# Half a product more before the bonus sums, and a decay scan in two pieces, in a two-block kernel on one Trainium2 core

## What is computed

```python
w_log = -jax.nn.softplus(-(w0 + jnp.tanh(pwd) @ w2)) - 0.5
decay = jnp.exp(-jnp.exp(w_log))          # cumulated over 64 tokens at a time by the kernel
a = jax.nn.sigmoid(a0 + pad_ @ a2)
k = pk * (1.0 + (a - 1.0) * k_a)
bonus = jnp.sum(r_h * k_h * r_k, axis=-1, keepdims=True) * v_h
_, sel = lax.top_k(score, topk)           # topk = 256
```

## Time and profile before

| | |
|---|---|
| median of 3 runs | 2707.3 us (2706.68 to 2709.66) |
| the profiled execution, its own time | 2704.38 us |
| its span on the core | 2702.6 us |
| busy PE, DVE, ACT, POOL in the whole span | 95%, 53%, 31%, 35% |
| the stage of the change, from the span's start | about 1567 to 2018 us |
| mean granted clock of PE over the span | 0.981 |

### The profile page before, as it was taken

The page is one execution under the profiler, slowest core; times in us unless marked ns, Lnnn a source line. Parts: engine busy times, 40 slices in busy tenths (PEclk is TensorE's granted clock), DMA queues, the critical chain, the costliest instruction groups (busy, mean ns, idle before and its releaser), DMA issues. The chain is left out here.

```text
span 2702.6 us, 40631 instructions
## 1 busy us (share of the span) xinstructions
PE 2557.4 (95%) x17201; PEld 2085.5 (77%) x17201; DVE 1441.9 (53%) x2106; ACT 849.2 (31%) x1393; POOL 947.9 (35%) x490
## 2 busy tenths in 40 slices
PE   7998999999999999998989999999999998899997
PEld 5887778888888888886867567777776778887786
DVE  5113543343342211223585689999975655565844
ACT  3304463321110111233432453533416541112331
POOL 3212333443342422444444025534512102121664
PEclk9999999999999999999999999999999999999999
DMA  3113213122222111112234014223322001101523
GB/s 130 48 41 109 94 40 108 48 87 82 83 83 93 49 39 50 52 47 86 78 102 148 32 34 131 94 90 121 110 90 97 17 26 71 35 4 58 186 71 109
DMA packets 82086, 207.67 MB, mean 77 GB/s; under 512 B 8393, under 2 KB 21745, under 8 KB 81905
## 3 DMA queue, kind: packets, MB, share of 16 engines
q1 hardware_dynamic: 74992, 192.48, 21.7%
q10 hardware_dynamic: 6912, 12.59, 1.2%
HBM read 170.81 MB, written 35.27 MB: 76 GB/s over the span
## 5 line engine op out<-in xcount | busy, mean ns | idle before, releaser
L332 PE MATMUL ps<-region_rounded,weights_hi_by_slot 128*128 128x512 f32 x2432 | 964.7, 397 | 32.2 <-DVE region_rounded L610 13.3
L333 PE MATMUL ps<-region_rounded,weights_hi_by_slot 128*128 128x512 f32 x2432 | 950.8, 391 | 0.0
L334 PE MATMUL ps<-region_rounded,weights_lo_in_place 128*128 128x512 f32 x2432 | 950.8, 391 | 0.0
L326 POOL TENSOR_TENSOR weights_lo_in_place<-wbuf,weights_hi_by_slot 128x1024 fp32r<-128x1024 f32 x194 | 486.0, 2509 | 735.2 <-ACT weights_hi_by_slot L322 735.2
L332 PEld LDWEIGHTS ps<-region_rounded,weights_hi_by_slot 128*128 128x128 f32 x2432 | 460.2, 189 | 137.3 <-issue 33.4
L333 PEld LDWEIGHTS ps<-region_rounded,weights_hi_by_slot 128*128 128x128 f32 x2432 | 460.1, 189 | 100.4 <-issue 6.1
L334 PEld LDWEIGHTS ps<-region_rounded,weights_lo_in_place 128*128 128x128 f32 x2432 | 459.4, 189 | 96.5
L322 ACT CAST weights_hi_by_slot<-wbuf 128x1024 fp32r<-128x1024 f32 x194 | 201.6, 1043 | 348.0 <-DMA wbuf<-w_mlp 219.5
L2065 DVE MAX8 gcols<-region 128x8 f32<-128x384 f32 (+5 forms) x192 | 171.5, 893 | 6.0
L2067 DVE MATCH_REPLACE8 region<-gcols,region 128x384 f32<-128x384 f32 (+5 forms) x192 | 168.1, 876 | 0.0
L1358 POOL TENSOR_TENSOR region_rounded<-region,region_rounded 128x512 fp32r<-128x512 f32 x64 | 83.1, 1298 | 214.6 <-DVE region_rounded L1502 214.6
(11 more groups left out here) (334 smaller groups left out, 3560.0 us busy)
## 6 DMA issues: line engine op xcount, KB each, us to landing
wbuf<-w_mlp SPq DMA_DIRECT2D x64, 512.0 KB, 3.6
wbuf<-w_hn SPq DMA_DIRECT2D x37, 512.0 KB, 4.0
wbuf<-w_in SPq DMA_DIRECT2D x25, 512.0 KB, 3.7
region<-xT SPq DMA_DIRECT2D x24, 512.0 KB, 6.5
xtra<-w_ada SPq DMA_DIRECT2D x32, 384.0 KB, 4.2
scratch_hn_out<-tmp ACTq DMA_DIRECT2D x48, 256.0 KB, 2.2
region<-scratch_hn_out SPq DMA_DIRECT2D x24, 512.0 KB, 8.2
wbuf<-w_att SPq DMA_DIRECT2D x20, 512.0 KB, 3.6
```

The lines of the kernel that those rows point to most:

```text
L326: self.nc.gpsimd.tensor_tensor(self.m.lo4[:, n % SLOTS, :], self.m.raw4[:, n % SLOTS, :], self.m.hi4[:, n % SLOTS, :].bitcast(F32), ALU.su ...
L332: nc.tensor.matmul(out, m.hi4[:, s, w], m.rounded(hi + k, half(hf)), start=(k == 0), stop=False)
L333: nc.tensor.matmul(out, m.hi4[:, s, w], m.rounded(lo + k, half(hf)), start=False, stop=False)
L334: return nc.tensor.matmul(out, m.lo4[:, s, w], m.rounded(hi + k, half(hf)), start=False, stop=(k == KT - 1))
```

## The change

Four things are done.

1. PE issues the two bonus sums of a program behind half product 8 of its count, not 7. ACT's L2013 and L2015 and POOL's L1887 to L1892 move by one half product too (8 to 9), and so do the stores on SP (9 to 10, 10 to 11).
2. `cumulate` makes two scans, of 896 and 128 columns, where it made 16 of 64. The scan computes state = keep * state + W. `keep` is 1 and is 0 at each 64th column, so the sum starts anew there. It lies in a part of the score area that the six blocks do not use. POOL waits for two scans instead of 16.
3. `keep` is written at the start of the stage by two MEMSETs on DVE, the second one (14 columns, 64 apart) behind a wait for the first.
4. DVE's jobs move to other rounds: clamps of programs 1 to 3 by 1, 2, 2 rounds, the inversions (with the scans) by 2 rounds each, the bonus products of all four by 4, 5, 4, 4 rounds.

```diff
-CLAMP_AT, INVERT_AT, BONUS_AT = [22, 75, 117, 153], [31, 81, 122, 158], [43, 91, 131, 165]
+CLAMP_AT, INVERT_AT, BONUS_AT = [22, 76, 119, 155], [31, 83, 124, 160], [47, 96, 135, 169]
...
+    keep_ready = S("keep_ready")
...
+    LONG = 14 * RL
+    keep = m.flat(SCORES, 4)[:, 25 * P:25 * P + LONG]
...
@@ sync
-                p = group_at(j, 9)
+                p = group_at(j, 10)
                 if p is not None:
                     sp.wait_ge(bonus_out, 2 * (p + 1))
...
-                p = group_at(j, 10)
+                p = group_at(j, 11)
                 if p is not None:
                     sp.wait_ge(rk_ready, p + 1)
...
@@ gpsimd
-                    pool.wait_ge(cum_ready, NC * 2 * (p + 1))
+                    pool.wait_ge(cum_ready, 2 * (p + 1))
...
-                p = group_at(j, 8)
+                p = group_at(j, 9)
                 if p is not None:
                     pool.wait_ge(e2_ready, p + 1)
...
@@ tensor
-                p = group_at(j, 7)
+                p = group_at(j, 8)
                 if p is not None:
                     pe.wait_ge(bonus_in, p + 1)
...
@@ vector
             def cumulate(p):
                 dve.wait_ge(lora_taken, 4 * (p + 1))
+                dve.wait_ge(keep_ready, 2)
                 if p:
                     dve.wait_ge(rb_ready, p)
-                for c in range(2 * NC):
-                    cols = slice(c * RL, (c + 1) * RL)
-                    nc.vector.tensor_tensor_scan(C[:, cols], m.const("ones")[:, 0:RL], W[:, cols], 0.0, ALU.mult, ALU.add
-                                                 ).then_inc(cum_ready, 1)
+                nc.vector.tensor_tensor_scan(C[:, 0:LONG], keep, W[:, 0:LONG], 0.0, ALU.mult, ALU.add).then_inc(cum_ready, 1)
+                nc.vector.tensor_tensor_scan(C[:, LONG:], keep[:, 0:T - LONG], W[:, LONG:], 0.0, ALU.mult, ALU.add
+                                             ).then_inc(cum_ready, 1)
...
             nc.vector.memset(S1[:, 0:1], 0.0).then_inc(consts_ready, 1)
+            nc.vector.memset(keep, 1.0).then_inc(keep_ready, 1)
+            dve.wait_ge(keep_ready, 1)
+            nc.vector.memset(keep[:, 0:LONG:RL], 0.0).then_inc(keep_ready, 1)
```

## The result

The changed kernel takes 2693.84 us, the median of 6 runs (2688.59 to 2694.75), beside 2706.99 us before (6 runs, 2704.14 to 2711.35). The ratio is 0.9942, 95% interval 0.9932 to 0.9952: faster by 0.6%, 13 to 18 us.

What follows compares the result with a forecast made beforehand. PE, busy 95%, was taken as the bound, its four stalls costing 18.4 us; less a 2.4 us wait left in program 3, 16.0 us go: 2707.3 - 16.0 = 2691.3 us, range 2687.5 to 2698.0.

Steps and rivals of the forecast that it cites:

- What a stall costs: PE's four waits before the bonus sums, with slower sums at the lower clock, lose 2.4 + 5.4 + 5.2 + 5.4 = 18.4 us.
- Part 1, the move: PE's bonus sums ask 5.44 us later; all else fixed, no wait is left and 18.4 us go, but lateness needs recomputing.
- The rival "no change": Scans save nothing, PE is tied to program 3, and rounds and L2070 give back the 5.44 won: 2708 us; chance 0.05.
- Part 2, the scans: On DVE, two long scans take 2.3 us with POOL quiet, saving 0.65 us; program 0 takes 4.7, saving 2.6.
- The sign of being wrong: On DVE, the prediction is wrong if long scans take over 2.1 ns a column beside a quiet POOL.
- Part 3, the ledger: PE's lateness by DVE's scans' end: -0.2, -1.0, +2.4 us in programs 1 to 3; PE gains 16.0 us.
- the rival of 10.9 us: DVE's L2070 of 640 columns falls behind POOL's L1890, costing 2.3 us; gain 10.9 us, 2696.4 us; chance 0.22.
- What costs nothing: MEMSETs, about 1.0 us, hide under DVE's 3.99 us wait at the first clamp; later ACT, POOL, SP steps delay nobody.
- The end: At the stage's end PE still finishes last, at 2001.6 us, 3.2 us behind DVE at 1998.4.

Runs made afterwards that it cites:

- the kernel with 158: Changed kernel with program 3's inversion at round 158, not 160: stage 435.56 us, median 2689.11, ratio 0.9930; run again, stage 434.22, median 2692.89, ratio 0.9933.
- the move alone: Kernel before with only the bonus sums' steps on PE, ACT, POOL and SP one half product later: stage 437.92 us, median 2694.16, ratio 0.9948.
- the kernel with the scans alone: Changed kernel with the order and all rounds of before, leaving the two long scans and MEMSETs: stage 448.86 us, median 2699.53, ratio 0.9969.

## Why the prediction was right

- **What a stall costs: right.** 18.4 us were counted from four stalls; with all waits gone the stage is 18.3 us shorter (the kernel with 158). The clock's share was real: only 12.5 of it stood as waits.
- **Part 1, the move: right, and more than I gave it.** I wrote that with all else fixed no wait would be left, but that DVE would not come forward with PE. It does come forward in part without any edit of DVE: its meetings with POOL vanish when POOL runs earlier. I used this for the changed kernel and did not ask what it meant for the move alone. Had the text gone one step further, it would have said that the long scans and the later rounds cancel. The rival "no change" made the same slip: it left the sets of 16 at their old 7.3, 3.0, 7.4 and 5.2 us. In the kernel with 16 scans at the new places they took 7.3, 3.0, 3.0 and 3.0, and the stage was still 7.0 us shorter than before.
- **Part 2, the scans: right in size.** 2.02 and 0.40 us against 2.0 and 0.4; program 0 cost 4.5 against 4.7, with the short scan at 2.55. A set of 16 takes 3.01 us from the first start to the last end, the pair 2.32: 0.69 saved, where the rows had given 0.65. (The rows' 2.07 ns a column give 2.12 us for 1024 columns, not the 2.17 in the sum; it changes nothing.) The sign of being wrong, over 2.1 ns a column, did not show if it is read as the slope, as it was derived: from 8 columns (0.165 us) to 896 (2.02) it is 2.09. The whole duration over its columns is 2.25. The estimate from the 58 cycles per instruction of the Trainium skill ("VectorE: DVE Perf Modes", section on the TRN2 errata) was 0.85; the runs are nearer to the rows.
- **Part 3, the ledger: right at its end, mixed on the way.** Program 3's wait was 2.16 us, 2.3 of lateness; its scans ended 8.65 us earlier than before, said 8.6. Programs 1 and 2 had more room than said: POOL's operand was ready 2.5 and 1.3 us before PE asked (said 0.2 and 1.0). Two meetings that hung on 0.1 us fell the other way: L2076 of 512 columns took 0.43 us, not 2.4, and that of 640 columns 2.60, where I had taken it free. The second is what the rival of 10.9 us was made of, but the first had given DVE 2.0 us and the second took 2.1, so the sum held. Two readings of the ledger were wrong and cancelled: its 0.1 us at program 3 is luck.
- **What costs nothing: right, with a term mis-sized.** The MEMSETs were put at 1.0 us; they cost 3.2. They pushed L2056, at 1572.29, behind the start of POOL's first L326 (1572.21, for 2.39 us), and it took 2.34 us instead of 0.16. Of the cover of 3.99 us at the first clamp 0.79 was left, and nothing of it in the two executions whose start was quicker by 1.6 us (last section). SP's and ACT's later steps held nobody up: PE has no other wait in the stage.
- **The end: right.** DVE ends 3.4 us ahead of PE, said 3.2.

The median is 2.5 us above the forecast. The stage is exact to 0.1, so the difference lies in the rest of the kernel. The same changed kernel reached the stage 1.9 us apart in its three profiled executions and took 3.2 us more or less behind it.

## What to carry to other kernels

A wait that a late operand causes is best priced per occurrence, as old lateness, less the work put in front of it, plus what the waiting engine has gained by then, less what the supplier has gained. The third term is the one that is forgotten, and it is what leaves a wait in the last of four programs that looks like the others. When an edit frees time on an engine off the path, ask what that time is spent on: here two later rounds in each of programs 1 to 3 gave all of it back, and 2.1 us more were to be had by not moving them.

## What the runs showed of the hardware that was not expected

**The clock does not fall at one length of idleness.** In the kernel with the scans alone PE idled 2.79 us and its sums took 1.98 us; it idled 2.67 us in the next program and they took 3.68. The granted clock in the first 2 us of these sums was 1.00 and 0.53. Of the waits before the bonus sums in all twelve profiled executions, all eight of up to 2.16 us kept the clock, and all six of 3.02 and more lost it. A wait of 3.02 us can keep it elsewhere, as the next paragraph shows.

**The stage's start is not always the same length.** After a wait of 3.02 or 3.03 us PE takes 30.60 to 30.65 us to its first head sums in ten of the twelve executions, 29.03 and 29.05 in two. The windows of the changed kernel and of the second one with 158 show the granted clock in the first 6 us:

```profile
1571.00:1577.00 6.00, 5.88 (x19) 4.74 (x20) 5.54 (x11) 1.05 (x1) 2.39 (x1) 0.72 0.07 22
```

```profile
1574.00:1580.00 6.00, 5.84 (x26) 4.85 (x27) 5.49 (x11) 1.13 (x2) 2.42 (x1) 1.00 0.10 25
```

It was 0.72 in the one and 1.00 in the other (and 0.72 and 1.00 over the same 6 us in the other executions too, by their start). The shift of 1.6 us is more than the 0.79 that the MEMSETs had left of DVE's cover: in both quick executions DVE does not wait at its first clamp, comes later than PE would have it, and so in program 0 POOL's L1864 starts before DVE's long scan (0.4 us before it in the kernel with the scans alone). The long scan takes 4.22 us in both, the pair 6.7; it takes 2.02 in every execution with the slower start, in which POOL's L1864 waits for it. POOL's timelines, first the changed kernel, then the one with the scans alone (a quick start):

```profile
1623.19 4.17 POOL L1864 TENSOR_TENSOR tmp<-tmp,xtra 128x1024 f32<-128x1024 f32 x1 [7.00 <-ACT xtra L1947]
```

```profile
1622.53 2.78 POOL L1864 TENSOR_TENSOR tmp<-tmp,xtra 128x1024 f32<-128x1024 f32 x1 [6.99 <-ACT xtra L1947]
1625.26 4.12 POOL L326 TENSOR_TENSOR weights_lo_in_place<-wbuf,weights_hi_by_slot 128x1024 fp32r<-128x1024 f32 x1
```

What decides the clock in each of these cases was not tried.
